# Latent attention in a hybrid trunk: each adaLN sum of a head's tick in two halves, the reciprocal between them

## What is computed

```python
c_act = jax.nn.silu(c)
for i in range(DEPTH):
    mod = c_act @ ada_w[i] + ada_b[i]
    sh_a, sc_a, g_a, sh_f, sc_f, g_f = [m[:, None, :] for m in jnp.split(mod, 6, axis=-1)]
    h = x * (1.0 + sc_a) + sh_a
    ...
    x = _layer_norm(DEEPNORM_ALPHA * x + (1.0 + g_a) * y, ln1_g[i], ln1_b[i])
```

```python
s = (einsum(q_nope, k_nope) + einsum(q_pe, k_pe)) * scale
p = jax.nn.softmax(jnp.where(mask, s, -jnp.inf), axis=-1)
outs.append(jnp.einsum('bhqk,bkhd->bqhd', p, v[:, :ke]))
```

## Time and profile before

| | us |
|---|---|
| median of 3 runs | 2195.82 (2195.4 to 2196.82) |
| profiled execution | 2195.4 |
| its span | 2193.6 |
| PE busy | 2139.0 |
| DVE busy | 1597.5 |
| ACT busy | 985.2 |

### The profile page before, as it was taken

How to read it: one execution, slowest core, us unless ns; L and a number is a source line. 1 busy time by engine, 2 the same in 40 slices (tenths; PEclk the granted TensorE clock), 3 DMA queues, 4 the chain that set the end, 5 groups by cost and what they waited for, 6 DMA issues and landing times.

```text
span 2193.6 us, 24790 instructions
## 1 busy us (share of the span) xinstructions
PE 2139.0 (98%) x9557; PEld 1744.2 (80%) x9557; DVE 1597.5 (73%) x1792; ACT 985.2 (45%) x1275; POOL 105.1 (5%) x208
## 2 busy tenths in 40 slices
PE   5799999999999999999999999999999999999999
PEld 2378887888888888888788888878888888888887
DVE  6789989787777777778887666878875555455566
ACT  1077635444443444443544455464444433444443
POOL 2101100000000000000000000000000000000000
PEclk9999999999999999999999999999999999999999
DMA  9999997889998898999588778958987665666673
GB/s 386 418 367 356 351 387 280 279 295 333 342 339 320 329 338 317 321 344 362 202 288 322 267 270 282 339 179 275 348 291 229 232 195 190 216 212 212 221 238 125
DMA packets 177064, 635.90 MB, mean 290 GB/s; under 512 B 20385, under 2 KB 51377, under 8 KB 150705
## 3 DMA queue, kind: packets, MB, share of 16 engines
q1 hardware_dynamic: 147298, 427.93, 56.0%
q0 software_dynamic: 27792, 201.34, 24.6%
q10 hardware_dynamic: 1856, 5.04, 0.6%
HBM read 616.37 MB, written 17.86 MB: 289 GB/s over the span
## 4 chain that ended last, share of the span: by engine, by line
PE 86%; DVE 6%; DMA 6%; ACT 1%; issue 1%; POOL 0%; SPq 0%; ACTq 0%; DVEq 0%; POOLq 0%
PE ps L1842 53%; PE ps L1848 27%; DMA ada_head<-in_ada_w 4%; PE ps L1859 3%; DMA raw<-in_mla_w_o 1%; DVE wlo L1150 1%; DVE ada_w L1187 1%; DVE ada_head L1187 1%; DVE ada_wide L1187 1%; DMA ada_w<-in_ada_w 1%; DMA raw<-in_mla_w_uv 0%; PE ps L2071 0%; DVE gate L1187 0%; PE ps L2101 0%; PE ps L2087 0%
## 5 line engine op out<-in xcount | busy, mean ns | idle before, releaser
L1150 DVE TENSOR_TENSOR wlo<-raw,whi 128x1024 fp32r<-128x1024 f32 (+1 forms) x717 | 867.2, 1216 | 515.1 <-ACT whi L708 514.3
L708 ACT ACTIVATE whi<-raw 128x1024 fp32r<-128x1024 f32 (+1 forms) x717 | 756.1, 1056 | 1054.8 <-PE ps L1848 968.5
L1842 PE MATMUL ps<-whi,hT_hi 128*128 128x512 f32 x1880 | 585.7, 393 | 0.6 <-DVE hT_lo L1577 0.6
L1842 PE MATMUL ps<-whi,hT_lo 128*128 128x512 f32 x1880 | 579.6, 389 | 0.0
L1848 PE MATMUL ps<-wlo,hT_hi 128*128 128x512 f32 x1880 | 502.7, 389 | 0.0
L1842 PEld LDWEIGHTS ps<-whi,hT_lo 128*128 128x128 f32 x1880 | 353.0, 188 | 74.0
L1848 PEld LDWEIGHTS ps<-wlo,hT_hi 128*128 128x128 f32 x1880 | 353.0, 188 | 73.6
L1842 PEld LDWEIGHTS ps<-whi,hT_hi 128*128 128x128 f32 x1880 | 350.2, 188 | 71.7 <-DVE hT_lo L1577 1.0
L1187 DVE CUSTOM_DVE_ANT_0 ada_w<-ada_w,c_bc,cols 128x2048 f32<-128x2048 f32 x145 | 339.8, 2345 | 14.3 <-ACT c_bc L1033 8.6
L1842 PE MATMUL ps<-whi,uT_lo 128*128 128x512 f32 x656 | 201.9, 389 | 0.0
L1842 PE MATMUL ps<-whi,uT_hi 128*128 128x512 f32 x656 | 201.9, 389 | 0.0
(11 more groups left out here) (271 smaller groups left out, 1463.1 us busy)
## 6 DMA issues: line engine op xcount, KB each, us to landing
raw<-in_ffn_w SPq DMA_DIRECT2D x528, 512.0 KB, 4.8
ada_w<-in_ada_w POOLq DMA_DIRECT2D x145, 1024.0 KB, 7.8
raw<-in_fox_w_in SPq DMA_DIRECT2D x96, 512.0 KB, 5.3
ada_head<-in_ada_w POOLq DMA_DIRECT2D x16, 1024.0 KB, 20.5
raw<-in_mla_w_o SPq DMA_DIRECT2D x32, 512.0 KB, 9.0
raw<-in_fox_w_o SPq DMA_DIRECT2D x32, 512.0 KB, 5.5
gate<-in_ada_w POOLq DMA_DIRECT2D x12, 1024.0 KB, 9.0
ada_low<-in_ada_w POOLq DMA_DIRECT2D x10, 1024.0 KB, 10.8
```

Source lines behind the costliest of these rows:

```text
L708: nc.scalar.activation(split_hi(pl.unit)[:, 0:n], raw[:, s, 0:n], ACT.Copy).then_inc(hi_ready, 1)
L1150: nc.vector.tensor_tensor(split_lo(pl.unit)[:, 0:n], raw[:, s, 0:n], split_hi(pl.unit)[:, 0:n].bitcast(F32), ALU.subtract).then_inc(lo_rea ...
L1842: nc.tensor.matmul(ps[:, 2 * pair + t, 0:width], a[:, t * P:(t + 1) * P], w_hi, start=(first and c == 0 and a is hi), stop=False)
```

## The change

In layer 0 the single ada sum is split into ada_first (columns 0 to 1023, starting from the bias) and ada_second (columns 1024 to 2047, starting from the value that the first half left in mod; it waits for ada_part, an own semaphore). The first half stands where the ada sum stood. The second half of the tick's first sum comes behind the split of gap 0 and ahead of the mask; that of the tick's second sum comes behind the split of gap 1 and behind the reciprocal, as the last instruction of the tick. The call for gap 2 falls away, which is empty in layer 0. Layer 1's order, the block before the ticks, the one after them, and all of ACT, PE, POOL and SP stay as they are.

```diff
+        ada_part = sem("ada_part")
...
+            def ada_first():
+                l, q, c = ADA_ORDER[pl.ada]
+                q += l * MODS
+                w = ada_buffer(pl.ada)[:, 0:D // 2]
+                dve.wait_ge(ada_in[ADA_SLOT[pl.ada]], 16 * ada_loads(pl.ada))
+                nc.vector.tensor_tensor_reduce(w, w, c_bc[:, 0:D // 2], 1.0, adab_col[:, q, c:c + 1],
+                                               ALU.mult, ALU.add, mod[:, q, c:c + 1]
+                                               ).then_inc(ada_part, 1)
+                pl.parts += 1
+
+            def ada_second():
+                l, q, c = ADA_ORDER[pl.ada]
+                q += l * MODS
+                w = ada_buffer(pl.ada)[:, D // 2:D]
+                dve.wait_ge(ada_part, pl.parts)
+                nc.vector.tensor_tensor_reduce(w, w, c_bc[:, D // 2:D], 1.0, mod[:, q, c:c + 1],
+                                               ALU.mult, ALU.add, mod[:, q, c:c + 1]
+                                               ).then_inc(ada_done, 1)
+                pl.ada += 1
...
+                    if layer == 0:
+                        again = i < TICKS - 1 and i not in (0, 2, 4)
+                        ada_first()
+                        gap(gaps[0])
+                        ada_second()
+                        if 1 <= i <= H:
+                            mask_scores(m)
+                        if again:
+                            ada_first()
+                        gap(gaps[1])
+                        if 1 <= i <= H:
+                            invert(m)
+                        if again:
+                            ada_second()
```

More of the change, by code:

```diff
@@ L133, in __init__ @@
         self.unit = self.pe = self.block = self.turn = self.turn_act = self.step = self.ada = 0
-        self.gate = self.halves = self.norm = 0
+        self.gate = self.halves = self.norm = self.parts = 0
 def pair_uses(block, pair):
@@ L1578, in o_low, with mask_scores, invert @@
                                             ).then_inc(o_lo, 1)
+                def mask_scores(m):
+                    dve.wait_ge(scored, m + 1)
+                    for t, a, b in ((0, 0, P), (1, P, 3 * P)):
+                        ins = nc.vector.tensor_tensor_reduce(
+                            p_sb[:, m % 2, a:b], ps[:, 5, a:b], mask[:, a:b], -scale,
+                            3.0e38, ALU.add, ALU.min, nmax[:, m % 2, t:t + 1])
+                    ins.then_inc(masked, 1)
+                def invert(m):
+                    dve.wait_ge(exp_done, m + 1)
+                    nc.vector.reciprocal(pinv[:, m % 2, :], psums[:, m % 2, :]).then_inc(inv_ready, 1)
@@ L1580, in attention @@
                 for i in range(TICKS):
                     gaps = tick_gaps(layer, i)
-                    g = H * layer + i
+                    m = H * layer + i - 1
                     if i >= 4:
                         o_low(i - 4)
[L1585 to L1603, removed]
+                    if layer == 0:
[12 more added lines that the diff above has]
+                            ada_second()
+                    else:
+                        if pl.ada < ada_end(1, SH_F):
+                            ada()
+                        gap(gaps[0])
+                        if 1 <= i <= H:
+                            mask_scores(m)
+                        if one_ada(i) and pl.ada < ada_end(1, SH_F):
+                            ada()
+                        gap(gaps[1])
+                        gap(gaps[2])
+                        if 1 <= i <= H:
+                            invert(m)
```

## The result

The changed kernel takes 2205.2 us in the median (2204.36 to 2208.64, 5 runs) against 2195.6 (2194.98 to 2196.82, 5 runs): 9.6 us or 0.44% slower by the medians. The ratio over all runs is 1.0047, with a 95% interval of 1.0037 to 1.0058. Forecast were 2202.1 and a range of 2197.3 to 2206.0. The five times fall into two groups, 2204.4 to 2205.2 and 2208.6; the profiled execution, with a span of 2206.9, is one of the slower two, so what its profile shows sums to more than the 9.6 us.

A forecast was written before the change was run, and what follows sets the result against it. PE was taken to bound the kernel, so only its stalls in layer 0's ticks count. Their growth summed to 6.9 us, less 0.6 for the loads, gave +6.3 and 2202.1 us; range 2197.3 to 2206.0.

The forecast's parts named there:

- The sign and the mechanism: In the ticks, later o_low lengthens PE's stalls one for one; slower, chance 0.60, by 6.3 us.
- The stalls, tick by tick: Additions to PE's stalls for o_low in ticks 4 to 18, each counted from the stall before; sum 6.9 us.
- the 0.1 of tick 14: At tick 14 o_low about 1 us late, which PE had about in hand: +0.1 us.
- The overhead of a pair: On DVE two halves cost 0.13 us more than a whole sum; 34 pairs, 4.4 us of DVE time.
- The waits for whi: DVE waits for whi behind halves that no longer cover it: 0.96, 0.6, 0.65 and 0.6 us.
- a stall of 3.3 us: PE's stall of 1.54 us at tick 4 grows to 3.3, as o_low(0) starts about 1.75 us later.
- The loads: Later ada loads at most +1.2 us, the wait for wlo in w_o gone at most -1.1; taken as -0.6.
- Only the overhead counts: Rival: the added waits for whi don't occur, pairs alone delay o_low; about +3 us, 2198.8; chance 0.20.
- The reciprocal was the path: Rival: an earlier reciprocal moves ACT's row up and shrinks stalls in ticks 8, 9, 10; about -2.5 us, 2193.3; chance 0.10.
- The ada loads get late: Rival: later buffer release holds loads between 250 and 330 us, DVE waits at several sums; 2206 to 2207; chance 0.08.
- The halves do nothing: Rival: the halves are spread so that all of it lies in slack; time as before; chance 0.02.

The follow-up runs named there:

- delay in tick 12: The kernel before with one extra DVE instruction of about 2.2 us ahead of o_low of tick 12; 2199.88 us, 3.9 over before.
- second sum whole: The changed kernel with each tick's second sum whole in its old place ahead of the split of gap 1; 2208.33 us, ratio 1.0061.
- reciprocal last: The changed kernel with the reciprocal behind the last half instead of ahead of it; 2212.86 us, ratio 1.0073.
- first attempt: The changed kernel with first sums whole, o_low ahead of the last half, and tick 8's second sum whole; 2196.63 us, ratio 1.0003.
- first sum whole: The changed kernel with each tick's first sum whole in its old place, the second split around the reciprocal; 2201.23 us, ratio 1.0027.
- second attempt: The kernel before with halves only for second sums of ticks 3, 5, 11 and tick 18's sum, next o_low ahead of the last half; 2197.88 us, ratio 1.0006.

## Why the prediction was right, and where it was short

**The sign and the mechanism.** PE is held in the ticks by o_low, and the change makes o_low later: shown by the waits, and by the kernel with o_low ahead of the last half, which loses 4.4 instead of 9.6 us.

**The stalls, tick by tick.** Forecast were additions of 1.75, 0.87, 1.0, 0.55, 0.5, 1.15 in ticks 4, 6, 8, 9, 10, 12 and, for tick 18, 0.95. The rows show 1.82, 0.89, 1.03, 0.60, 0.66 (before it was too small to be marked) and 1.17, and for tick 18 0.80 (1.60 against 0.21 and 0.59). Together 7.0 against 6.9; the 0.1 of tick 14 didn't come. A part of the 1.82 is chance: o_low(0) starts 1.63 us later (174.28 against 172.65), and PE happened to reach it 0.19 us earlier than in the profile before.

**The overhead of a pair.** 0.13 us holds for halves with work between them; the kernel with both together shows 0.26. The table with 58 cycles of the VectorE: DVE Perf Modes page of the Trainium skill (section on the errata), by which I estimate 0.06 us, is too low for both. The same section's note has about 150 cycles, by which I estimate 0.16 us; that is 2.6 times the table, not double as the prediction has it, and closer to the measured 0.13. The finding of the same page of the Trainium skill under "The DRAIN you can't avoid", that in a chain of copies a semaphore after each one adds nothing, does not carry over to an operation that waits for the accumulated sum of the one right ahead of it: 1.32 against 1.20 us from start to start.

**The waits for whi.** In tick 3 0.90 us (0.96 forecast; by the rows that it names, 168.14 less 167.21, it should have been 0.93), in tick 5 0.50 (0.6), shown by their rows and by the kernel in which these two sums are whole. In ticks 6 and 10 they are 0.57 and 0.52 (0.65 and 0.6).

**The step that was short: what a stall costs.** I priced a stall at its length, and left the clock out, although the forecast named a stall of 3.3 us where the longest in the ticks before was 1.54. The granted clock fell behind three of the stalls in the profiled execution, at 1.5 to 1.8 us each, 4.9 us in all. The single delay of 2.2 us cost 3.9 in the median, and its profile has 2.19 of stall and 1.6 of clock. For the median of the changed kernel, stalls of 7.0 us and one or two such falls would make 8.6 or 10.2; it is 9.6. Which of it a median execution has isn't shown, since the profiled one is the slowest of the five.

That the measured time lies in the range is in part luck. The upper end, 2206.0, was put there for the case of late ada loads, which did not come; nothing in the range was meant for the clock.

**The loads.** Forecast was -0.6 for w_o. PE's wait of 1.1 us for wlo there is gone in the changed kernel, as forecast, but behind it PE waits 0.88 us for xa, where it had no such wait. The same matmul of the norm starts 11.96 us later than before (356.09 against 344.13), as much as the stalls and the clock had already cost by the end of the ticks (7.0 and 4.9): the gain did not arrive.

**The rivals.** "Only the overhead counts" at +3: refuted by the waits for whi and by the timeline. "The reciprocal was the path": the reciprocal did come earlier, but ACT's wait fell by 1.6 us only, to 6.2 where the forecast said under 4, and no stall of PE shrank. "The ada loads get late": no wait of DVE for ada_w among its waits in the ticks. "The halves do nothing": the interval of the ratio excludes it.

## What to carry to other kernels

A long instruction between a result and its use on another engine may be cover: before it is cut, look at what its successor waits for and how long that chain is on the other engine, in every repetition of the loop, and not only where the trace now shows a wait. Count what stands ahead of the one instruction that the bounding engine waits for; a piece that is moved behind a result that helps nobody and ahead of that instruction costs its full length. Where two engines are within 0.2 us of each other, a wait put down to one is a wait for both, and mending one moves the stall to the next place. Give a stall of the matrix engine of about 2 us or more a fall of the clock on top, as a chance and not as a certainty: here 11 of 15 stalls of 2 us or more in the ticks had one.

## What the runs showed of the hardware

The granted clock fell to its lower level behind stalls in PE's work that is dense otherwise, and stayed there for about 3 us. In these profiles it fell after stalls of 1.96, 2.04 and 3.36 us (the changed kernel), 1.92 and 2.87 (halves together), 2.15 (o_low earlier), 2.24 and 2.02 (whole in ticks 3 and 5), 3.06 (delay in tick 12), 3.99 (second sum whole), and 4.13, 2.62 and 3.18 (reciprocal last). Behind the ticks it fell once more, after a wait of 1.78 us for wlo in w_o (first attempt). It stayed up after 1.81, 1.80 and 1.90 (first sum whole), 1.76 (halves together), 1.84 (o_low earlier), 1.94 (whole in 3 and 5) and 1.97 (second attempt), and also after 2.33, 2.88 and 2.72 in the kernel with the second sum whole and after 3.29 in the one with the reciprocal last. No stall of the kernel before, up to 1.54 us, is followed by a fall in the ticks. The moment varies: behind tick 8 of the changed kernel the clock was up for another 1.1 us after the stall, in tick 4 it fell 0.3 us before the stall was over. So length alone doesn't decide, and what else does is open here. Nor is the scatter of the times explained by these falls: the kernel before, whose profile has none in the ticks, took 2194.6 to 2200.9 us in 23 executions, as wide a spread as any of the others.

An instruction of DVE that waits for its predecessor's accumulated sum starts 0.11 us later than one that doesn't, 1.32 against 1.20 to 1.21 us from start to start for 128 x 1024 (halves together).
